# Three of eight key and value tiles of the second memory attention, computed in the first expert stage instead of in the first mixer's cell

## What is computed

```python
def mem_cross_attention(hn, mem_n, wq, wkv, wo):
    q = (hn @ wq).reshape(bsz, seq, XATTN_HEADS, XATTN_HEAD_DIM)
    k, v = jnp.split(mem_n @ wkv, 2, axis=-1)     # 256x1024 @ 1024x2048
    ...
def peer_ffn(hn, wq, subkeys, u_tab, v_tab):
    q = (xt @ wq).reshape(T, PEER_HEADS, 2, PEER_HALF)
    s = jnp.einsum('thpd,hpkd->thpk', q, subkeys)
    ...                      # two top-16 searches, a top-16 of their sums
    ub = u_tab[ib]           # 16 expert rows per token and head
    vb = v_tab[ib]
    act = gelu(einsum('td,thkd->thk', xb, ub))
    return einsum('thk,thkd->td', gb * act, vb)
```

## Time and profile before

| what | value |
|---|---|
| median of three runs | 3461.26 us |
| runs | 3452.0, 3463.8, 3461.26 us |
| span of the profiled execution, first to last instruction | 3449.7 us |
| median of the runs less that span | 11.6 us |
| mean granted clock of TensorE | 0.922 |
| busy: TensorE, VectorE, ScalarE, GpSimd | 84%, 71%, 22%, 18% |
| moved by DMA | 859.85 MB, 249 GB/s on average |

### The profile page before, as it was taken

How to read it: one execution, slowest core, us unless ns; L and a number is a source line. 1 busy time by engine, 2 the same in 40 slices (tenths; PEclk the granted TensorE clock), 3 DMA queues, 4 the chain that set the end, 5 groups by cost and what they waited for, 6 DMA issues and landing times. The chain is left out here.

```text
span 3449.7 us, 44738 instructions
## 1 busy us (share of the span) xinstructions
PE 2883.2 (84%) x17440; PEld 2263.9 (66%) x17440; DVE 2461.4 (71%) x4655; ACT 773.6 (22%) x1985; POOL 620.8 (18%) x520
## 2 busy tenths in 40 slices
PE   8789977777777889677777779998887999998898
PEld 8578863333333689333333329997777999987798
DVE  7262677777776886877777878777346877868686
ACT  4124122222222342222222221013223101013300
POOL 0000014444445100444444440000000000000000
PEclk9999988898899999898998879999988999999999
DMA  6363569999999735899999995644113555652364
GB/s 207 101 188 98 190 220 421 412 420 410 405 410 421 258 111 178 355 409 417 411 419 392 408 396 172 192 153 135 47 60 125 171 184 166 188 176 86 123 196 141
DMA packets 469122, 859.85 MB, mean 249 GB/s; under 512 B 18736, under 2 KB 398512, under 8 KB 402224
## 3 DMA queue, kind: packets, MB, share of 16 engines
q0 software_dynamic: 73728, 536.90, 37.8%
q1 hardware_dynamic: 394896, 319.85, 29.4%
q10 hardware_dynamic: 288, 0.24, 0.0%
HBM read 848.55 MB, written 8.39 MB: 248 GB/s over the span
## 5 line engine op out<-in xcount | busy, mean ns | idle before, releaser
L2436 PE MATMUL banks<-arena,arena 128*128 128x512 f32 x1744 | 913.6, 682 | 353.4 <-ACT arena L2505 353.3
L2436 PEld LDWEIGHTS banks<-arena,arena 128*128 128x128 f32 x1744 | 371.6, 220 | 876.6 <-ACT arena L2505 438.6
L2394 POOL DMA_INDIRECT arena<-in_peer_uv,arena x512 | 615.8, 1203 | 1371.4 <-DVE arena L2622 673.3
L2660 DVE CUSTOM_DVE_ANT_0 arena<-arena,normed 128x1024 f32<-128x1024 f32 x512 | 626.1, 1223 | 231.9 <-DMA arena<-in_peer_uv,arena 229.2
L410 DVE TENSOR_TENSOR weight_ring_part<-weight_ring,weight_high_parts 128x2048 fp32r<-128x2048 f32 (+2 forms) x244 | 539.8, 2212 | 8.4
L3214 PE MATMUL banks<-normed_columns_part,weight_high_parts 128*128 128x256 f32 x1408 | 396.5, 282 | 2.8 <-DVE weight_ring_part L410 2.2
L3215 PE MATMUL banks<-normed_part,weight_high_parts 128*128 128x256 f32 x1408 | 394.1, 280 | 0.0
L3216 PE MATMUL banks<-normed_columns_part,weight_ring_part 128*128 128x256 f32 x1408 | 394.0, 280 | 0.0
L754 PE MATMUL banks<-weight_high_parts,arena_part 128*128 128x256 f32 x1216 | 344.0, 283 | 35.2 <-PEq L350 23.4
L407 DVE CAST weight_high_parts<-weight_ring 128x2048 fp32r<-128x2048 f32 (+2 forms) x244 | 289.8, 1188 | 107.4 <-PE banks L756 87.8
L755 PE MATMUL banks<-weight_ring_part,arena_part 128*128 128x256 f32 x1216 | 341.6, 281 | 0.0
(11 more groups left out here) (573 smaller groups left out, 4274.4 us busy)
## 6 DMA issues: line engine op xcount, KB each, us to landing
weight_ring<-in_ffn_w_gate SPq DMA_DIRECT2D x88, 512.0 KB, 3.7
weight_ring<-in_ffn_w_up SPq DMA_DIRECT2D x88, 512.0 KB, 4.8
weight_ring<-in_ev_w_in SPq DMA_DIRECT2D x33, 1024.0 KB, 5.3
weight_ring<-in_ffn_w_down SPq DMA_DIRECT2D x32, 1024.0 KB, 5.2
weight_ring<-in_od_w_in SPq DMA_DIRECT2D x23, 1024.0 KB, 5.3
weight_ring<-in_xa_wkv SPq DMA_DIRECT2D x16, 1024.0 KB, 5.3
weight_ring<-in_peer_wq SPq DMA_DIRECT2D x16, 1024.0 KB, 5.3
weight_ring<-in_ev_w_out SPq DMA_DIRECT2D x12, 1024.0 KB, 5.6
```

The lines of the kernel that those rows point to most:

```text
L2394: pool.indirect_dma_start(out=ring[:, slot(i, s), :], out_offset=None, in_=table, in_offset=bass.IndirectOffsetOnAxis(ap=index[:, i % 2, s ...
L2436: mm = pe.matmul(k.ps[:, 2 * b + half, :], diag[:, g % 2, s, :], v, start=n == b * PEER_TOPK, stop=n == last_mixed[b])
L2660: dve.tensor_tensor_reduce(out=ring[:, here, 0:D], in0=ring[:, here, 0:D], in1=k.xn[:, i % NB, :], scale=1.0, scalar=0.0, op0=ALU.mult, op ...
```

## The change

Tiles 5, 6 and 7 of the eight of the second attention's keys and values (all three are values) leave the cell. In the order of weights they stand after the first two query tiles of the first expert stage. There TensorE multiplies them after the scores of head 1 and before the first row is mixed, in banks 2 and 3, which the mixing of block 1 uses from the second turn on. ScalarE evicts each side into one buffer of 128 x 256 (`wide`), and each eviction after the first waits until the store before it has landed. SyncE fetches the memory again, once the gain row has been read, stores the six sides, and issues the next query tile after each second store. TensorE waits for all six evictions before it mixes the first row of the second turn; VectorE waits for the last two stores near the end of the stage.

```diff
+LATE, LATE_BANK = 3, 2
+        self.late = {0: ("01", range(8 - LATE, 8), self.kept_memory)}
...
+    def feed_to(self, sp, last):
+        taken, self.taken = self.taken, last - RING
+        self.feed(sp)
+        self.taken = taken
+
+    def store_late(self, sp, s):
+        sp.wait_ge(self.side_out.sem, s + 1)
+        sp.dma_start(self.side[s][4], self.wide[:, :]).then_inc(self.side_stored[s % STAGES].sem, 16)
+        self.side_stored[s % STAGES].adds(16)
+
+    def late_stored(self, e, s):
+        e.wait_ge(self.side_stored[s % STAGES].sem, 16 * (s // STAGES + 1))
+
+    def keep_late(self, act, sides):
+        for s in sides:
+            act.wait_ge(self.side_done.sem, s + 1)
+            if s > sides[0]:
+                self.late_stored(act, s - 1)
+            act.activation(self.wide[:, :], self.ps[:, LATE_BANK + s % SIDE_BANKS, 0:WIDTH], ACT.Copy).then_inc(self.side_out.sem, 1)
+            self.side_out.adds(1)
...
@@ def attention(l):   # weight_order
-        add(tiles_of(ins["peer_wq"][l], 0, 2 * D))
+        queries = tiles_of(ins["peer_wq"][l], 0, 2 * D)
+        add(queries[0:2])
+        add_whole(late_tiles(ins, l))
+        add(queries[2:])
@@ weight_order
-    add_whole(tiles_of(ins["xa_wkv"][1], 0, 2 * D))
+    add_whole(tiles_of(ins["xa_wkv"][1], 0, 2 * D)[0:8 - LATE])
@@ mlstm, SyncE
-            k.store_side(sp, range(s0, s0 + 16), feed=True)
+            k.store_side(sp, range(s0, s0 + 10), feed=True)
@@ mlstm, TensorE
-            k.multiply_side(pe, u0 + 14, u0 + 24)
+            k.multiply_side(pe, u0 + 14, u0 + 18)
             turn_out(0)
-            k.multiply_side(pe, u0 + 24, u0 + 32)
+            k.multiply_side(pe, u0 + 18, u0 + 20)
             turn_out(1)
@@ mlstm, ScalarE
-            k.keep_side(act, range(s0 + 7, s0 + 9))
+            k.keep_side(act, range(s0 + 7, s0 + 8))
             square(1)
             take_root(1)
-            k.keep_side(act, range(s0 + 9, s0 + 12))
+            k.keep_side(act, range(s0 + 8, s0 + 9))
             keep_columns(0)
-            k.keep_side(act, range(s0 + 12, s0 + 16))
+            k.keep_side(act, range(s0 + 9, s0 + 10))
             keep_columns(1)
@@ select_and_mix
+    extra = LATE if l in k.late else 0
+    k.taken += PEER_HEADS + extra
+    queries = [first + h + (extra if h >= 2 else 0) for h in range(PEER_HEADS)]
...
@@ select_and_mix, SyncE
+            if extra:
+                k.feed_to(sp, first + 4)
+                sp.wait_ge(k.tile_out.sem, k.tile_out.start + NB)
+                sp.dma_start(memT, kept_memory).then_inc(k.memory_in.sem, 16)
+                k.memory_in.adds(16)
+                k.feed_to(sp, first + 6)
+                for s in sides:
+                    k.store_late(sp, s)
+                    if s % 2:
+                        k.feed_to(sp, first + 6 + (s - s0) // 2 + 1)
             k.feed(sp, ahead=2)
@@ select_and_mix, TensorE, behind scores(1)
+            if extra:
+                pe.wait_ge(k.memory_in.sem, memory_loaded)
+                k.multiply_side(pe, u0, u0 + 4 * extra, bank_at=LATE_BANK)
...
             for g in range(len(groups)):
+                if extra and g == per_group:
+                    pe.wait_ge(k.side_out.sem, s0 + 2 * extra)
                 mix(g)
@@ select_and_mix, ScalarE
             raise_top(0)
+            k.keep_late(act, sides)
@@ select_and_mix, VectorE, near the end
+            for s in sides[-2:]:
+                k.late_stored(dve, s)
             add_tiles(1, range(tiles))
```

More of the change, by code:

```diff
@@ L450, in weights, with begin_memory @@
         return self.tile(self.high, at % HIGH, n), self.tile(self.ring_low, n % RING, n)
-    def begin_memory(self, name, memT):
+    def begin_memory(self, name, memT, tiles=None, first=None):
         keys, vals = self.kept[name]
-        first = self.side[-1][0] + 1 if self.side_units < 2 * len(self.side) else self.taken
+        if first is None:
+            first = self.side[-1][0] + 1 if self.side_units < 2 * len(self.side) else self.taken
         half = keys.shape[1] * P // WIDTH
-        for t in range(2 * half):
-            n = first + t
+        for at, t in enumerate(range(2 * half) if tiles is None else tiles):
+            n = first + at
             assert n in self.whole
@@ L499, in store_side, with multiply_side @@
                 self.feed(sp)
-    def multiply_side(self, pe, first, last):
+    def multiply_side(self, pe, first, last, bank_at=CHAIN):
         for u in range(first, last):
@@ L511, in multiply_side @@
             w = self.tile(self.ring, n % RING, n)
-            bank, cut = self.ps[:, CHAIN + s % SIDE_BANKS, 0:WIDTH], slice(j * P, (j + 1) * P)
+            bank, cut = self.ps[:, bank_at + s % SIDE_BANKS, 0:WIDTH], slice(j * P, (j + 1) * P)
             for c in range(u % 2 * HALF, u % 2 * HALF + HALF):
@@ L1206, in tiles_of, with late_tiles @@
             for c in range(col0, col1, width) for k in range(0, rows, KC)]
+def late_tiles(ins, l):
+    return tiles_of(ins["xa_wkv"][1], 0, 2 * D)[8 - LATE:] if l == 0 else []
 def weight_order(ins):
@@ L1751, in mlstm @@
                also=fetch_memory, vector_then=convolve_rest)
-    k.begin_memory("01", memT)
+    k.begin_memory("01", memT, range(8 - LATE))
     u0, s0 = k.side_units, k.side_units // 2
@@ L2326, in select_and_mix @@
     first = k.taken
-    k.taken += PEER_HEADS
+    extra = LATE if l in k.late else 0
+    k.taken += PEER_HEADS + extra
+    queries = [first + h + (extra if h >= 2 else 0) for h in range(PEER_HEADS)]
     for h in range(PEER_HEADS):
-        k.tile_freed[first + h] = (k.produced, k.produced.start + 2 * (h + 1))
+        k.tile_freed[queries[h]] = (k.produced, k.produced.start + 2 * (h + 1))
+    u0, s0 = k.side_units, k.side_units // 2
+    sides = range(s0, s0 + 2 * extra)
+    assert k.side_units == 2 * len(k.side)
+    memT = k.gain_memory[:, :, :]
+    if extra:
+        name, which, kept_memory = k.late[l]
+        k.begin_memory(name, memT, which, first + 2)
+        k.side_units = 2 * len(k.side)
+        memory_loaded = k.memory_in.total + 16
     high_x, low_x = parts
@@ L2403, in query @@
                     pe.wait_ge(k.query_kept.sem, k.query_kept.start + h - 1)
-                w_high, w_low = k.weights(pe, first + h)
+                w_high, w_low = k.weights(pe, queries[h])
                 for j in range(2):
```

## The result

The kernel after took 3470.15 us, the median of 20 runs, the one before 3461.21 (20 runs beside them). The ratio is 1.0027, interval 1.0019 to 1.0035: 9.3 us slower, 6.6 to 12.1. The forecast was 3467.6, +6.3. Run again beside other kernels it was 1.0021 (1.0008 to 1.0035), 7.3 us slower.

What follows compares the result with a forecast made beforehand. The cell was taken as TensorE-bound, the expert stage as DMA-bound. From 3461.3 us, less 15.6 for the cell, plus 21.9 for the stage (10.3 bytes, 11.6 empty time), gives 3467.6 us; range 3452 to 3477.

Steps and rivals of the forecast that it cites:

- The cell: TensorE-bound cell: six sides leave, VectorE's splits then hold its end; 15.9 us earlier, gain 15.6 us (13 to 16).
- The chain in the expert stage: Expert stage: evictions wait for stores queued among loads and gathers, so first gelu moves from 505.78 to 531.5, delaying the eleventh gather.
- the store among gathers: Expert stage: a store takes 2.1 us alone, plus 2.8 us as an eighth of a 22.6 us load.
- the share of query tile 2: Expert stage: an estimated 0.3 MB of query tile 2, pushed past 492, stands ahead of the first store in SyncE's queue.
- The bytes: DMA-bound expert stage: 4.05 MB more at 2.55 us each cost 10.3 us, bounds 0 and 11.5.
- The empty time: Expert stage: between 521 and 540 the DMA engines have 7.4 us of work, so 11.6 us are empty.
- 1, the stores pass quickly: Expert stage: evictions follow TensorE's 3.46 us, no empty time, only bytes; -5.3, 3456 us; chance 0.25.
- 2, the lateness passes through whole: Expert stage: the ring doesn't refill at once; 25.5 us plus about 5 for bytes; +15, 3476 us; chance 0.12.
- 3, free bytes: Expert stage: the DMA share hides slack and the stores pass too; -15.6 + 0 to 3, 3447 us; chance 0.08.
- 4: Cell gives less, only 8 us, through a late output-matrix load or slow clock; stage pays 21.9; 3475 us; chance 0.05.
- The rule on ring order: SyncE's queue: transfers share one ring per DMA engine, consumed in order, so a small store can't overtake a load.
- the estimate of 23 us per load: DMA engines alternating queues packet by packet: 1 KB of load beside 8 KB of gather, nine times 2.55 us.

Runs made afterwards that it cites:

- dropped run: Kernel after, with the three late tiles left out altogether, neither loaded nor multiplied, and the memory not fetched again: 3442.41 us, ratio 0.9954 to the kernel before.
- after, again: The kernel after, unchanged, run once more beside other kernels on one chip: 3464.17 us, ratio 1.0021 to the kernel before.
- stores first: Kernel after, with SyncE issuing query tiles 2 and later only behind the six stores: 3466.40 us, ratio 1.0026 to the kernel before.
- three, parked: Kernel after, with all six sides multiplied before any eviction, held in PSUM, then evicted each to its own place without waiting for stores: 3453.55 us, ratio 0.9985.
- the last two kernels: The parked three-tile kernel with VectorE's splits ahead of its first low parts, 3447.99 us, and the kernel after run again beside it, 3464.17 us.
- no stores: Kernel after, without its six late stores and with evictions not waiting for any; loads and multiplications stay: 3453.78 us, ratio 0.9983 to the kernel before.
- loads-only run: Kernel after, loading the three tiles and fetching the memory in the expert stage, without multiplying, evicting or storing: 3453.24 us, ratio 0.9988 to the kernel before.

## Why the prediction was right

**The cell** was right to a few tenths. With the 0.57 us taken off by which the cell began later, the turns come at 326.1 and 330.5 (326.1 and 330.4 forecast) and the next block 16.05 us earlier (15.9), held by VectorE; the medians of the dropped run give 15.9. The 0.3 us for the half clock is too small to be told. From the next block's start to the first gather it took 133.4 us before, 133.1 after, 133.3 in "after, again" and 134.7 in the dropped run.

**The chain in the expert stage** was right in kind and nearly in size. In the old times: first eviction 493.3 (494), second 501.2 (503.5), third 509.4 (509), fourth 524.2 (524.4), last 531.4 (531.5), gelu 533.1 (531.5), eleventh gather 538.0 (537 to 538.6). It was a little luck. Two terms were off and cancelled: the store among gathers was put at 4.9 us and took 7.5 to 8.6, and the share of query tile 2 ahead of the first store was put at 4 us of delay but wasn't felt, for in "stores first", where it isn't ahead, the second eviction comes 8.6 us after the first, in the kernel after 8.0.

**The terms of the stage's sum.** The bytes were put at 10.3 us. "Three, parked" gives 8.3 or 13.0 by the profile, as one takes the dropped run or the kernel before for the stage without them, and 10.7 by the ratios. That agrees with 10.3 and can't test it finer. The empty time was put at 11.6 us. The DMA engines show 13.1, and 13.4 in "after, again"; the stages less that of "three, parked" give 15.4 and 11.7, the ratios (1.0027 less 0.9985) 14.5, and so do the medians of the last two kernels. So this term was too small, by 1.5 to 3 us, and the end of the pause is where I was off. I had it from 521 to 540 in the old times with 7.4 of 19 us filled. It lasted from 521.8 to 543.8 (506 to 528; from 504 to 506 they still moved 372 GB/s) with 9 of 22 filled. The engines ran empty about when I said, but were full again only 5.8 us after the eleventh gather, where I had allowed 2.

Together the stage paid 23.7 to 28.4 us in the profile after and 20.0 to 24.7 in "after, again"; by the medians it paid 25.2 (9.3 + 15.9) or 23.2 (7.3 + 15.9). The sum was 21.9. The result came 3 us above the forecast, inside its range, and 1 us above in the repeat. The first interval (6.6 to 12.1) leaves the forecast of +6.3 just outside, the second (2.8 to 12.1) holds it.

**The rivals.** 1, the stores pass quickly, is what "no stores" and "three, parked" are, and came out at 3454 to 3456 as worked out (3456); with the stores in one buffer it didn't occur. 2, the lateness passes through whole: half right. From the eleventh gather to the last dot the kernel after took 645.5 us and 641.6 in the repeat, the kernel before 642.2 and the dropped run 647.4, so the 25 us of lag did pass through. What failed of it is the further 5 us of bytes, which had been moved in the pause. It is the same loss counted from the other end, and no backlog of VectorE is needed for it: the DMA engines were back at 411 GB/s by 532. 3, free bytes, is out by the loads-only run, 4 by the dropped one.

**The rule on ring order**, the Trainium skill, "DMA: Bandwidth & Descriptors", section "Queues, rings and completion order": the store behind query tile 3 landed in 14.3 us, without it in 8.6. It came in 0.4 us after that load, which had taken 21.7 (issued at 486.27). The section keeps this order for the completion signal on each DMA engine, and not for the data. The rule fits, but this doesn't prove it: in both kernels the third store landed just as the DMA engines ran empty, 33.8 us behind the first gather in the kernel after and 28.5 in "stores first", and the two loads that the kernel after has more by then are 5.1 us of bytes. It was not the larger part: in "stores first", with nothing of SyncE's ahead, the four waits for stores still add up to 26.6 us, here to 32.2. The estimate of 23 us per load takes one row of 1 KB against one of 8 KB; the section lets an engine drain a packet of several descriptors before it switches, so the estimate stands only if both queues have as many in one, and no run here shows that.

## What to carry to other kernels

Work that fills one engine's idle time also needs a way out: ask where its results go, and how long a buffer is held when it is freed by a store in a stage where the DMA engines are full. Leaving results in PSUM until the critical instruction has gone, and giving each its own place, turned a loss of 7 to 9 us into a gain of 5 (0 to 10) with the same matmuls and bytes, and of 10 with VectorE's splits put first. Moving bytes from a stage that has room to one bound by bytes is paid at about that stage's rate, here 8 to 13 us for 4 MB, and has to be set against the gain from the start. A price of a few us in one stage wants more than one profile of that stage: two of the same code differed here by 4.7.

## What the runs showed of the hardware

A store of 128 KB took 1.9 to 2.1 us with nothing beside it and 7.5 to 8.6 us beside up to ten outstanding gathers of 1 MB; a load of 1 MB took 5.3 and 21.7 us. The eighth of the size thus doesn't take an eighth of the delay: an eighth of 21.7 on top of 2.1 would have been 4.8. Behind a load that was itself among gathers it took 14.3.

TensorE stood idle 4.48 us before the fifth side and 9.34 before the sixth. They took 5.41 and 6.72 us where a side at full clock takes 3.5. The granted clock was 0.53 to 0.62 between 494 and 498, and 0.50, 1.2 of 2.4 GHz, from 505 to 514. The idle time just before doesn't settle it alone: in "stores first" a side behind 2.19 us of idle took 5.41 and the next one, behind 2.55, took 3.72.
